# Moving the combine matmuls of a routed FFN from the gate/up phase to the down phase, and one output row block to GpSimd

## The reference, cut to what matters

```python
def expert_choice_ffn(h, w_router, w_gate, w_up, w_down):
    probs = softmax(h @ w_router)                 # (512, 16)
    gate, idx = lax.top_k(probs.T, 64)            # each expert takes 64 tokens
    xs = h[idx]                                   # (16, 64, 1024)
    a = einsum('ecd,edf->ecf', xs, w_gate)        # f = 2048
    u = einsum('ecd,edf->ecf', xs, w_up)
    y = einsum('ecf,efd->ecd', silu(a) * u, w_down) * gate[..., None]
    return segment_sum(y, idx)                    # back to (512, 1024)

# second_block, at its end
x = x + expert_choice_ffn(rms_norm_2(x, norm2_g), w_router, w_gate, w_up, w_down)
return rms_norm_2(x, final_g)
```

## Time and profile before

| | us |
|---|---|
| median of 3 runs | 2081.55 (2080.7 to 2082.39) |
| the profiled execution, its own time | 2081.55 |
| its span in the trace | 2080.1 |
| PE busy | 1863.6 (90% of the span) |
| DVE busy | 491.8 (24%) |
| ACT busy | 272.3 (13%) |
| POOL busy | 33.9 (2%) |

### The profile page before, as it was taken

How to read it: one execution, slowest core, us unless ns; L and a number is a source line. 1 busy time by engine, 2 the same in 40 slices (tenths; PEclk the granted TensorE clock), 3 DMA queues, 4 the chain that set the end, 5 groups by cost and what they waited for, 6 DMA issues and landing times.

```text
span 2080.1 us, 19253 instructions
## 1 busy us (share of the span) xinstructions
PE 1863.6 (90%) x8342; PEld 750.9 (36%) x8342; DVE 491.8 (24%) x978; ACT 272.3 (13%) x478; POOL 33.9 (2%) x44
## 2 busy tenths in 40 slices
PE   8999999979999969999995999988888888888886
PEld 4444444443333325545443333322222223222222
DVE  3566001241001026990124011111011111110112
ACT  3322000121010114402201100000000000000001
POOL 0000000010000010000000000000000000000000
PEclk9999999979999989999997999999999999999999
DMA  6221032456998881211256899999999999999996
GB/s 235 81 81 41 0 121 81 179 192 259 387 389 348 372 304 68 82 41 61 95 212 263 328 428 428 428 428 427 428 427 428 427 428 428 428 428 427 427 428 278
DMA packets 68537, 589.80 MB, mean 284 GB/s; under 512 B 5472, under 2 KB 6880, under 8 KB 37216
## 3 DMA queue, kind: packets, MB, share of 16 engines
q1 hardware_dynamic: 59904, 556.55, 64.8%
q10 hardware_dynamic: 4448, 17.28, 2.1%
q0 software_dynamic: 4096, 14.68, 2.1%
HBM read 575.91 MB, written 12.58 MB: 283 GB/s over the span
## 4 chain that ended last, share of the span: by engine, by line
PE 55%; DMA 36%; DVE 6%; issue 2%; ACT 1%; SPq 0%; POOL 0%; ACTq 0%; DVEq 0%
PE ps L252 23%; DMA ring<-in_w_up 21%; DMA ring<-in_w_down 9%; PE ps L2175 8%; PE ps L1032 7%; DMA ring<-in_exp_w_up 5%; PE ps L2201 5%; PE ps L661 3%; PE ps L1820 3%; PE ps L261 2%; PE ps L583 1%; PE ps L1712 1%; PE ps L2157 1%; DMA AR<-h_rows,AR 1%; PE ps L276 0%
## 5 line engine op out<-in xcount | busy, mean ns | idle before, releaser
L252 PE MATMUL ps<-AR,ring 128*128 128x512 f32 x1160 | 503.3, 595 | 4.9 <-DVE AR L2033 3.6
L252 PEld LDWEIGHTS ps<-AR,ring 128*128 128x128 f32 x1160 | 220.5, 191 | 280.7 <-issue 275.9
L2175 PE MATMUL ps<-ring,AR 128*64 128x512 f32 x1008 | 233.5, 607 | 43.8 <-DMA ring<-in_w_up 32.0
L1032 PE MATMUL ps<-ring,AR 128*32 128x512 f32 x1536 | 257.9, 623 | 12.6 <-DMA ring<-in_exp_w_up 10.0
L2313 DVE TENSOR_TENSOR XT<-XT,ps 128x512 f32<-128x512 f32 x128 | 82.0, 684 | 785.0 <-PE ps L2157 785.0
L2175 PE MATMUL ps<-AR 128*64 128x512 f32 x1040 | 235.2, 597 | 33.1 <-DMA AR<-in_w_up 23.5
L1032 PE MATMUL ps<-AR 128*32 128x512 f32 x768 | 164.2, 593 | 0.0
L2175 PEld LDWEIGHTS ps<-ring,AR 128*64 128x64 f32 x1008 | 69.1, 138 | 205.2 <-issue 119.7
L2175 PEld LDWEIGHTS ps<-AR 128*64 128x64 f32 x1040 | 71.6, 136 | 188.8 <-issue 120.7
L2201 PE MATMUL ps<-ring,AR 128*64 128x512 f32 x512 | 122.9, 628 | 6.7 <-DMA ring<-in_w_down 5.9
L1032 PEld LDWEIGHTS ps<-ring,AR 128*32 128x32 f32 x1536 | 72.5, 114 | 140.8 <-issue 140.3
(11 more groups left out here) (350 smaller groups left out, 1040.1 us busy)
## 6 DMA issues: line engine op xcount, KB each, us to landing
AR<-in_w_gate SPq DMA_DIRECT2D x33, 2048.0 KB, 33.6
ring<-in_w_up SPq DMA_DIRECT2D x32, 2048.0 KB, 35.4
AR<-in_w_up SPq DMA_DIRECT2D x32, 2048.0 KB, 33.5
ring<-in_w_down SPq DMA_DIRECT2D x32, 2048.0 KB, 35.4
AR<-in_w_down SPq DMA_DIRECT2D x32, 2048.0 KB, 35.4
ring<-in_w_gate SPq DMA_DIRECT2D x31, 2048.0 KB, 33.9
ring<-in_w_in SPq DMA_DIRECT2D x15, 2048.0 KB, 8.3
ring<-in_exp_w_up SPq DMA_DIRECT2D x15, 2048.0 KB, 13.7
```

The source lines that it names most:

```text
L252: x = PE.matmul(ps, l, r, start=i == 0, stop=i == len(pairs) - 1)
L1032: yield k, c, PE.matmul(b[32 * c:32 * c + 32, :], rows(k), w(k), start=k == 0, stop=k == nk - 1, tile_position=(0, 32 * c), skip_group_che ...
L2175: x = PE.matmul(GU[2 * m + f // 2][64 * (f % 2):64 * (f % 2) + 64, :], XS[n // 2 % 2][:, k * P + 64 * b:k * P + 64 * b + 64], w[:, kk_, f ...
```

## The change

It does five things.

- PE: `combine(n-1, c)` moves from behind chunk pair c of the gate/up phase to ahead of `cd{n}.c` in the down phase, and `rows` from the middle of the gate/up phase to its end.
- PE and ACT: both halves of the transposed product go through one bank, 5. The second half, and the first one of the next expert, wait for ACT's copy.
- ACT: the silu of one column goes.
- DVE: the two products come ahead of the adds of the expert before.
- The end: DVE takes the reciprocal of row block 0 ahead of the last two adds; POOL multiplies that block, in two operations, and SP's first output DMA waits for POOL. DVE does the other three.

```diff
-        HB = (TR, CO[1])
...
@@ pe_choice
                         x.then_inc(e_gu, 1)
-                    if n:
-                        combine(n - 1, c)
-                    if c == 1 and b == 0 and n + 2 < 16:
-                        rows(n // 2 + 1)
+                if b == 0 and n + 2 < 16:
+                    rows(n // 2 + 1)
                 for f in range(2):
                     PE.wait_ge(d_he, 2 * n + f + 1)
                     if f == 0:
                         PE.wait_ge(a_xs, 2 * min(n // 2 + 2, 8))
-                    elif n:
-                        PE.wait_ge(d_co, 8 * n)
-                    transposes(HB[f], [cHE[b][:, f * T + s:f * T + T:4] for s in range(4)]).then_inc(e_ht, 1)
+                        if n:
+                            PE.wait_ge(a_hb, 2 * n)
+                    else:
+                        PE.wait_ge(a_hb, 2 * n + 1)
+                    transposes(TR, [cHE[b][:, f * T + s:f * T + T:4] for s in range(4)]).then_inc(e_ht, 1)
                 for c in range(4):
+                    if n:
+                        combine(n - 1, c)
                     w, s, v = weights(f"cd{n}.{c}", 4)
                     PE.wait_ge(s, v)
                     if c == 0:
-                        PE.wait_ge(a_hb, 2 * n + 1)
-                    elif c == 2:
                         PE.wait_ge(a_hb, 2 * n + 2)
+                        if n:
+                            PE.wait_ge(a_ye, n)
...
@@ act_choice
             rows(0)
-
-            AC.activation(q4[:, 1, :], eps, ACT.Silu)
             AC.wait_ge(s_h2e, 64)
...
-                                  HB[f][:, :].rearrange("p (s h t) -> p s h t", s=4, h=2), ACT.Copy).then_inc(a_hb, 1)
+                                  TR[:, :].rearrange("p (s h t) -> p s h t", s=4, h=2), ACT.Copy).then_inc(a_hb, 1)
...
@@ dve_choice
+                for f in range(2):
+                    DV.wait_ge(a_si, 2 * n + f + 1)
+                    DV.tensor_tensor(cHE[b][:, sl(f)], cHE[b][:, sl(f)], GU[2 + f][:, :], ALU.mult).then_inc(d_he, 1)
                 if n:
                     for a in range(4):
                         combine(n - 1, a)
-                for f in range(2):
-                    DV.wait_ge(a_si, 2 * n + f + 1)
-                    DV.tensor_tensor(cHE[b][:, sl(f)], cHE[b][:, sl(f)], GU[2 + f][:, :], ALU.mult).then_inc(d_he, 1)
...
             for a in range(4):
                 combine(15, a)
+                if a == 2:
+                    inverse(0)
             DV.wait_ge(s_p3, 32)
-            for a in range(4):
+            for a in range(1, 4):
                 inverse(a)
-                DV.wait_ge(f_y, 2 * a + 1)
+                DV.wait_ge(f_y, Y_R[a])
...
+        Y_R, Y_Y = (1, 2, 4, 6), (None, 3, 5, 7)
...
@@ pool_choice
+            PO.wait_ge(s_p3, 32)
+            PO.wait_ge(f_y, Y_R[0])
+            PO.tensor_scalar(XK[:, 0:D], XK[:, 0:D], ss[:, 0:1], None, ALU.mult).then_inc(s_po, po())
+            PO.wait_ge(s_po, po.n)
+            PO.tensor_tensor(XK[:, 0:D], XK[:, 0:D], gn, ALU.mult).then_inc(s_po, po())
...
@@ sp_choice
-            for a in range(4):
-                SP.wait_ge(f_y, 2 * a + 2)
+            SP.wait_ge(s_po, po.n)
+            SP.dma_start(out[0, 0:P, :], XK[:, 0:D]).then_inc(s_out, 16)
+            for a in range(1, 4):
+                SP.wait_ge(f_y, Y_Y[a])
                 n = D if a < 3 else T
                 SP.dma_start(out[0, a * P:(a + 1) * P, 0:n], XK[:, a * D:a * D + n]).then_inc(s_out, 16)
-
-            SP.wait_ge(f_y, 9)
+            SP.wait_ge(f_y, Y_Y[3] + 1)
```

## The result

The changed kernel takes 2094.48 us (median of 4 runs, 2093.39 to 2095.94), the one before 2081.54 (4 runs, 2080.7 to 2082.39) on the same chip. The ratio is 1.0062, 95% interval 1.0045 to 1.0080: +12.9 us, 9.4 to 16.6. The forecast was +6.7, its range ended at 2092.0. The profiled execution took 2092.64 us, its span is 2091.1, that is 11.0 above the span of before.

The account below looks back on a forecast made before the run. The DMA weight stream was taken to bound the middle, so only its start and what follows its last chunk could change the time: 3.4 + 0 + 2.7 + 0.6 = +6.7 us on 2081.55, 2088.3 us, range 2084.0 to 2092.0.

Parts of the forecast that it names:

- step 3: Last down phase, expert 15: combine matmuls now stand where PE must catch up, 4.64 us per chunk for 3.44; +2.7 us.
- step 4: The end: SP's first output DMA waits for POOL, taken at 3.35 us, part made up in writing out; +0.6 us.
- three signs of being wrong: Load behind `cd0.0` before 1188 us, PE catching up within the last down phase, or POOL taking over 5 us.
- Step 1: Expert 0: late `rows(1)`, table load and one-bank turns delay `cd0.0`, and so the weight stream's start; +3.4 us.
- Step 2: Experts 1 to 14: PE's work per expert stays under 58.9 us, so the weight stream hides the moves; 0 us.
- rival of 0.20: Expert 15's boundary: PE's clock falls to its lower level there too; +1.7 us, 2090.0 us in all; chance 0.20.
- bound of +4.4: Last down phase: upper bound on its cost if the clock falls as at expert 0, 1.7 us more.
- upper bound, 6.7 us for POOL: The end: three passes for each of POOL's two operations, 3.35 us more than taken, all handed on; bound +4.3 us.
- POOL against DVE: The end: POOL's product advances only beside no DVE work, ends 4.2 us later than taken; 2092.4 us; chance 0.10.

Follow-up runs that it names:

- the kernel with the move alone: Kernel before with the combine matmuls moved to the down phase and DVE's products ahead of its adds: +6.2 us (4.0 to 8.5) against before.

## Why the prediction was wrong

The sign was right, and so were the three places and what waits for what there. Two terms of the sum were mis-sized, the last down phase (step 3) and POOL's work at the end (step 4), and step 4 had one overlap wrong. Of its three signs of being wrong one came true: POOL took over 5 us.

- **Step 1, +3.4 forecast.** 3.9 in the profile. The chain came as written; the half us on top is the product's two turns at the lower clock (3.66 us and not 2.98). `cd0.0` itself was taken at the loss of before, and in the two profiles compared that held (5.36 and 5.35 us). That the delay passes on one to one holds in every kernel: the stream took 854.8 to 855.5 us wherever the queue had run dry, and 856.2 to 856.3 where the next load came before that.
- **Step 2, 0 forecast.** Held: -0.4.
- **Step 3, +2.7 forecast, 4.2 in the profile.** This term was mis-sized. The 2.7 is right at full clock (2.55 measured with two banks). What failed is the choice of the full clock. The lower clock at that boundary stood as a rival of 0.20, argued down since expert 15 before showed none, and as the bound of +4.4, which the 4.2 nearly met. It fell at that boundary or in the down phase behind it in 12 of the 13 other profiles (all but the changed kernel with two banks). With two banks and the combine where it was, the last down chunk stands 0.2 to 0.7 us later in the profiles with a fall (19.77, 19.87 and twice 20.23 us from last up to last down chunk, against 19.54), because PE, needing 3.44 us a chunk that takes 4.91 to come, still catches up. The change spends this reserve, and then the fall is paid: some 1.5 us in the changed kernel (23.74 against the 22.27 that the prediction's terms give at full clock, 2064.2 less 2041.95, an estimate), 3.2 in the kernel with the move alone. So a profile of before without a fall said little about the kernel after.
- **Step 4, +0.6 forecast, 3.5 in the profile.** This term was mis-sized too, and by more. 3.35 us were taken for POOL's work; it took 5.9. The scaling of one tensor, taken for one pass like the iota's (1.12 us), costs 2.85; the product, taken for two passes (2.23), costs 2.34 alone, so that part was sized well, and 0.7 more beside DVE. So the first output went out 3.6 us later and not 0.95. That writing out would make up for up to 0.8 of a late start also failed: it made up for 0.1. From the first output DMA to the end it is 6.6 to 7.0 us in every kernel of the table, whether the others were ready long before or came one by one. The end moves with the first output, one to one. The upper bound, 6.7 us for POOL, did hold the 5.9; the value chosen within the bounds was what failed, and no row of before held such an operation.
- **POOL against DVE, 0.10.** Half right: the two do slow each other, yet POOL's product took 0.7 us longer for it and not 4.2, and it was DVE that came off worse (3.30 us for 1.41), off the path to the first output.

With the measured sizes the sum is 3.9 - 0.4 + 4.2 + 3.5 = 11.2 of the 12.9 us (9.4 to 16.6). What the rest is stays open. The likeliest is the clock in `cd0.0`: over the profiles with the same start the first column averages 35.9 us for the changed kernel (four) and 30.6 for the one before (two), 5.3 apart and not 3.9, an estimate. That would be 1.4 of the missing 1.7, but six profiles are too few to show it.

## What to carry to other kernels

Where a stream bounds a stretch, moved work is free in its middle and dear at its last item: what the consumer needs per item must stay clearly under what one takes to arrive, or every disturbance shortly ahead of the end is paid in full. Where its queue has run dry, the start of such a stream is set by the first buffer that comes free late, so nothing may be put on the chain that frees it. And an in-order queue of output DMAs begins when its first item is ready, so the first block shouldn't go to the slowest engine. Whether POOL could take a later block without loss wasn't tried; its two operations take 5.2 us alone, DVE's multiplication of a block with its reciprocal 1.4.

## What was not expected of the hardware

POOL's multiplication of one 128x1024 tensor by a value per row took longer (2.85 us) than its product of two tensors (2.34 us alone). DVE's multiplication of two 128x512 pieces with two SBUF inputs took 3.30 us beside POOL's product and 1.41 without, nearly all of the difference in the first piece (2.64 us); beside POOL's scaling the same instruction on 1024 columns took its usual 1.28.
